# Scores of two attention stages: fp32 products on 64 rows become two fp32r products on 128 rows, with queries and keys stored as rounded part and remainder

## The chip, the cores and the metric

The program runs on one core of a Trainium2 chip, as one launch. The time is device microseconds of that launch, the median of several runs. The core has TensorE (PE, matmuls; PEld is its weight loads), VectorE (DVE), ScalarE (ACT), GpSimd (POOL), SyncE (SP), and 16 DMA engines that serve the queues of SP and POOL. SBUF has 128 partitions, of which TensorE contracts over up to 128 (its rows); PSUM takes the products.

## The reference, cut to what matters

The whole is a chain of layers over 1024 tokens and a context of 256 (1280 together). The change lies in the first mixer, which has two kinds of attention with heads of 64:

```python
# A: 8 query heads, 2 key heads (4 queries share a key head), a window of +-128 tokens plus the context, a sink column
s = einsum(qg, k) * 64**-0.5 ; s = where(valid, s, -1e30)
p = softmax(concat([s, sink]))[..., :-1] ; out = p @ v
# B: 4 heads, each two softmaxes over all 1280 keys
w = softmax(q1 @ k1.T * 64**-0.5) - lam * softmax(q2 @ k2.T * 64**-0.5) ; out = w @ v
```

q and k are normalised per head (RMS), gained, and rotated (RoPE) before. The context's own tokens attend to the context alone.

## The kernel before, in words

**project_even** (line 626 on) multiplies the normalised input with the weights, 80 steps of 24 matmuls of 128x416 (8 blocks of columns, 10 tiles of 128 tokens). Beside it, per tile i from step 33 + 4i on (`turn_at`), a side job makes q and k: SP loads 26 heads back (`qk`), ACT squares them, DVE reduces, normalises, gains and rotates them (into one of two buffers `rot`), PE transposes 14 chunks of 128x128 at step `turn_at(i) + 6` into PSUM (`pt`), ACT copies them to `stage` (L773, `copy_out`) at the next tile's `turn_at + 3`, and SP stores `stage` to DRAM as `rT` (L726, `out_stage`) at `turn_at` of the tile after. `stage` has 14 chunks because the two key heads of A are written twice, so that each stands on both partition halves. SP also loads in each step a slab of another weight (L736), which DVE multiplies and adds (L867, L870, `terms`), and stores the step's result (L753). Each queue runs in program order.

**attention_even** (line 914 on) runs 70 units: six for the two context tiles (`dac`, `wac`), then 32 pairs of `da` (kind B, one head of one tile of 128 queries: two score rows of 1280 keys) and `wa` (kind A, two heads: 384 near keys with a mask added by a product, and 256 context keys). At its start SP and POOL load keys `KA`, `KB`, values `va`, `vb` and queries `qT`, all of them for the whole sequence and with 128 partitions a DMA: the even head of a pair lies on partitions 0 to 63, the odd one on 64 to 127. A score product (L1261, L1273, L1279 to L1282, L1291) is an fp32 matmul over 64 rows; two heads on the two halves stand in turn. PE's order by hand, for unit u: transposes of exp'd scores of unit u-2 (`turn`, L1301), products with the values (`multiply`, L1324), and in between the scores of u (`score`), in two parts. `da` writes its scores into both PSUM tiles `pS`, part 0 (keys 0 to 512) before the first transposes of u-2 and part 1 (the rest) behind them; `wa` uses `pS[0]` alone, both parts behind the first transposes. Score part 0 of `wa` waits for the exp of the `da` before it to have read `pS[0]` (`expd`), and that of `da` for the first exp of `wa`. DVE takes the maxima (L1131, L1137), ACT the exp (L1083, L1088) and the copies of the transposes out of PSUM (L1108). On ACT the three copies of u-2 stand ahead of the exps of u.

In PE's waits, unit 0 needs `kb_ctx_in` and `q_ctx_in`, unit 6 (the first `da` of the sequence) `keys_in` and `q0_in`, unit 7 `ka_in`. POOL's side job (sums, L1040, L1047) begins when `q1_in` has come.

The later stage forgetting_attention (line 2662 on, tiles `fx_`) is not touched by the change; it already makes scores as two fp32r products on 128 rows (L2857, L2858), and it loads `fx_ks`, `fx_qc` and `fx_kc` by DMAs of 64 partitions with rows of 4 KB (L2735 to L2737).

Of the kernel before, what the change touches and what calls it, by code (L numbers as in the profile page):

```python
# [11 lines left out]
P = 128  # L12
D = 1024
KD = D // P
SEQ = 1024
# [610 lines left out]
def project_even(nc, a, g, hT, raw, first, p0, rT, sums):  # L626
# [29 lines left out]
    with Phase(nc, "p0") as ph:  # L656
# [8 lines left out]
        rot = [ph.sb(f"rotated{s}", [P, 28, HD]) for s in range(2)]  # L665
        ss = ph.sb("ss", [P, QK_HEADS])
        rt = ph.sb("rt", [P, QK_HEADS])
        stage = ph.sb("stage", [P, 14, P])
# [7 lines left out]
        small, squared, summed, rooted, recips, normed, gained, spread, rotated, turned, evac, stage_out = ph.sems(  # L676
            "small squared summed rooted recips normed gained spread rotated turned evac stage_out")
# [11 lines left out]
        with nc.Block() as block:  # L689
# [15 lines left out]
            def _(sp):  # L705
# [53 lines left out]
                sp.wait_ge(stage_out, 16 * n_all)  # L759
# [3 lines left out]
            def _(act):  # L763
# [5 lines left out]
                def copy_out(i):  # L769
                    act.wait_ge(turned, i + 1)  # L770
                    if i:
                        act.wait_ge(stage_out, 16 * i)
                    act.activation(stage[:, :, :], pt[:, 0:14, :], ACT.Copy).then_inc(evac, 1)  # L773

                def side():
                    for i in range(n_all):
# [3 lines left out]
                        if i >= 2:  # L780
                            act.wait_ge(turned, i - 1)
                        act.activation(rot[s][:, 0:QK_HEADS, :], qk[s][:, :, :], ACT.Square).then_inc(squared, 1)
# [25 lines left out]
            def _(dve):  # L808
# [6 lines left out]
                def side():  # L815
                    for i in range(n_all):
# [5 lines left out]
                        dve.tensor_reduce(ss[:, :], rot[s][:, 0:QK_HEADS, :], AX.X, ALU.add).then_inc(summed, 1)  # L822
# [13 lines left out]
                        if i:  # L836
                            dve.wait_ge(rotated, i)
                        cos = rope[:, 0, i:i + 1, :]
                        dve.tensor_tensor(rot[s][:, 0:8, :], qk[s][:, 0:8, :], cos.broadcast_to([P, 8, HD]), ALU.mult)
                        for y in range(2):  # L840
                            dve.tensor_tensor(rot[s][:, 8:12, :].rearrange("p (k r) d -> p k r d", r=2)[:, :, y, :],
                                              qk[s][:, 8:10, :], cos.broadcast_to([P, 2, HD]), ALU.mult)
                        dve.tensor_tensor(rot[s][:, 12:28, :], qk[s][:, 10:26, :], cos.broadcast_to([P, 16, HD]), ALU.mult)
# [9 lines left out]
                        dve.tensor_tensor(rot[s][:, 0:8, :], rot[s][:, 0:8, :], tmp[:, 0:8, :], ALU.add)  # L853
                        for y in range(2):
                            keys = rot[s][:, 8:12, :].rearrange("p (k r) d -> p k r d", r=2)[:, :, y, :]
                            dve.tensor_tensor(keys, keys, tmp[:, 8:10, :], ALU.add)
                        dve.tensor_tensor(rot[s][:, 12:28, :], rot[s][:, 12:28, :], tmp[:, 10:26, :], ALU.add).then_inc(rotated, 1)
# [26 lines left out]
            def _(pe):  # L884
                def side():
                    for i in range(n_all):
                        yield turn_at(i) + 6
                        pe.wait_ge(rotated, i + 1)
                        if i:
                            pe.wait_ge(evac, i)  # L890
                        for c, at in enumerate((0, 1, 2, 3, 8, 9, 4, 5, 6, 7, 10, 11, 12, 13)):
                            mm = pe.transpose(pt[:, at, :], rot[i % 2][:, 2 * c:2 * c + 2, :].rearrange("p h d -> p (h d)"), g.ident[:, :])
                        mm.then_inc(turned, 1)
# [20 lines left out]
def attention_even(nc, a, g, rT, p0, o_dram, sums):  # L914
# [10 lines left out]
    QA, KA_AT, QB, KB_AT = 0, 8, 4, 10  # L925
# [34 lines left out]
    with Phase(nc, "att") as ph:  # L960
        qT = ph.sb("qT", [P, KD, ALLT])
        KA = ph.sb("KA", [P, 2, P + ALLT])
        KB = ph.sb("KB", [P, 4, ALLT])
# [25 lines left out]
        (small, padded, cast, signed, scores, banked, topped, negmax, expd, sink_in, sinked, joined, summed, recips, ratioed,  # L989
         weights, turned, evac, values, o_done) = ph.sems(  # L990
            "small padded cast signed scores banked topped negmax expd sink_in sinked joined summed recips ratioed "
# [5 lines left out]
        keys_in, vb_in, ka_in, va_in, q0_in, q1_in = ph.sems("keys_in vb_in ka_in va_in q0_in q1_in")  # L997
        kb_ctx_in, ka_ctx_in, q_ctx_in, vb_ctx_in, va_ctx_in = ph.sems("kb_ctx_in ka_ctx_in q_ctx_in vb_ctx_in va_ctx_in")
# [8 lines left out]
        with nc.Block() as block:  # L1007
            @block.sync
            def _(sp):
                sp.dma_start(KB[:, :, SEQ:], rT[KB_AT:KB_AT + 4, :, SEQ:].rearrange("c p t -> p c t")).then_inc(kb_ctx_in, 16)  # L1010
                sp.dma_start(KA[:, :, P + SEQ:], rT[KA_AT:KA_AT + 2, :, SEQ:].rearrange("c p t -> p c t")).then_inc(ka_ctx_in, 16)
                sp.dma_start(vb[:, NT:, :], p0[SEQ:, V_B:V_B + 512].rearrange("(t p) d -> p t d", p=P)).then_inc(vb_ctx_in, 16)
                sp.dma_start(va[:, 1 + NT:, :], p0[SEQ:, 640:768].rearrange("(t p) d -> p t d", p=P)).then_inc(va_ctx_in, 16)
                sp.dma_start(KB[:, :, 0:SEQ], rT[KB_AT:KB_AT + 4, :, 0:SEQ].rearrange("c p t -> p c t")).then_inc(keys_in, 16)
                sp.dma_start(vb[:, 0:NT, :], p0[0:SEQ, V_B:V_B + 512].rearrange("(t p) d -> p t d", p=P)).then_inc(vb_in, 16)
                sp.dma_start(va[:, 1:1 + NT, :], p0[0:SEQ, 640:768].rearrange("(t p) d -> p t d", p=P)).then_inc(va_in, 16)
                sp.dma_start(qT[:, :, 2 * P:SEQ], rT[0:8, :, 2 * P:SEQ].rearrange("c p t -> p c t")).then_inc(q1_in, 16)
                for tile in tiles_in_order:
                    sp.wait_ge(o_done, last_of[tile] + 1)
# [5 lines left out]
            def _(pool):  # L1025
                for h in (slice(QB, QB + 4), slice(QA, QA + 4)):
                    pool.dma_start(qT[:, h, SEQ:], rT[h, :, SEQ:].rearrange("c p t -> p c t")).then_inc(q_ctx_in, 16)
# [3 lines left out]
                pool.dma_start(qT[:, :, 0:2 * P], rT[0:8, :, 0:2 * P].rearrange("c p t -> p c t")).then_inc(q0_in, 16)  # L1031
                pool.dma_start(KA[:, :, P:P + SEQ], rT[KA_AT:KA_AT + 2, :, 0:SEQ].rearrange("c p t -> p c t")).then_inc(ka_in, 16)
                pool.memset(va[:, 0, :], 0.0).then_inc(padded, 1)
                pool.memset(KA[:, :, 0:P], 0.0).then_inc(padded, 1)
# [24 lines left out]
                pool.wait_ge(q1_in, 16)  # L1059
# [183 lines left out]
            def _(pe):  # L1243
                warm_up(pe, g, po, 20)
                def score(u, part):
# [11 lines left out]
                    q = slice(P * token_tile(u), P * token_tile(u) + P)  # L1257
                    if kind == "da":
                        for c0, c1 in ((0, 512),) if part == 0 else ((512, 1024), (1024, ALLT)):
                            for m, half in enumerate(halves):  # L1260
                                mm = pe.matmul(pS[m][:, c0:c1], qT[half, QB + j, q], KB[half, j, c0:c1], start=True, stop=True)  # L1261
                                if c1 == ALLT:
                                    mm.then_inc(scores, 1)
                    elif kind == "wa":
# [4 lines left out]
                        left = [qT[half, QA + j, q] for half in halves]  # L1269
                        right = [KA[half, kv, :] for half in halves]  # L1270
                        if part == 0:
                            for e in range(2):
                                pe.matmul(pS[0][:, KEYS * e:KEYS * e + W3], left[e], right[e][:, near], start=True, stop=False)  # L1273
                            for e in range(2):
                                edges = pS[0][:, KEYS * e:KEYS * e + W3].rearrange("p (b k) -> p b k", b=3)[:, 0:3:2, :]
                                mm = pe.matmul(edges, unit_r[:, :], mask[:, which, :, :], start=False, stop=True)
                            mm.then_inc(banked, 1)
                            return
                        pe.matmul(pS[0][:, W3:512], left[0], right[0][:, far:far + P], start=True, stop=True)  # L1279
# [2808 lines left out]
```

## Time and profile before

| | us |
|---|---|
| median of 3 runs | 3462.72 (3462.21 to 3463.39) |
| span of the profiled execution | 3460.9 |
| PE busy in it | 3176.7 (92%) |
| DVE / ACT / POOL busy | 1711.3 (49%) / 1221.1 (35%) / 298.4 (9%) |

The span runs from the first to the last instruction of one profiled execution; what the runs count beyond it is 1.8 us by their median. project_even ends and attention_even begins at about 459 us, the first unit of the sequence is at 504.8 us and the last ends at about 890 us. A busy share is an average over stages; matmul records overlap in time, so the distance from one start to the next tells the cost and not the duration.

### The profile page before, as it was taken

How to read it: one execution, taken by the hardware profiler on the slowest of the kernel's cores; microseconds unless marked ns; L12 is line 12 of the kernel's file. 1: busy time of each engine (PE TensorE's matmuls, PEld its weight loads, DVE VectorE, ACT ScalarE, POOL GpSimd, SP SyncE). 2: the span in 40 equal slices, each digit the busy share in tenths (PEclk: the TensorE clock that was granted, in tenths of full speed). 3: DMA queues.
4: the chain of work that ended last, by engine and by line, in shares of the span. 5: the costliest groups of instructions: out<-in, count | busy, mean ns of one | idle time of the engine just before them, and what ended most of it. 6: DMA issues, size and time to landing. Idle time of an engine off the chain costs nothing. (4 is left out here: it accounts for less than half of the span.)

```text
span 3460.9 us, 51322 instructions
## 1 busy us (share of the span) xinstructions
PE 3176.7 (92%) x20902; PEld 2807.3 (81%) x20902; DVE 1711.3 (49%) x2697; ACT 1221.1 (35%) x2257; POOL 298.4 (9%) x357
## 2 busy tenths in 40 slices
PE   7999979999798999897999997979988999999988
PEld 4999967777587999775888976767856999999877
DVE  3459736666472211265526216746645445454343
ACT  4313235666562343124534114544423111111232
POOL 1000011100010000111211100002200000000010
PEclk9999999999899999998999998989999999999999
DMA  5556560000443221234211335110022111112332
GB/s 185 162 179 226 182 215 20 25 13 13 159 156 95 79 78 60 99 119 143 102 47 41 93 99 138 38 7 2 3 86 79 49 48 42 48 46 73 99 133 92
DMA packets 199262, 309.34 MB, mean 89 GB/s; under 512 B 43016, under 2 KB 133896, under 8 KB 197020
## 3 DMA queue, kind: packets, MB, share of 16 engines
q1 hardware_dynamic: 178448, 232.54, 21.1%
q0 software_dynamic: 20624, 74.13, 6.6%
q8 instruction: 136, 2.23, 0.3%
q14 instruction: 54, 0.44, 0.0%
HBM read 229.80 MB, written 76.81 MB: 89 GB/s over the span
## 5 line engine op out<-in xcount | busy, mean ns | idle before, releaser
L115 PE MATMUL p_pb<-p_w_hi,h_hi 128*128 128x416 f32 (+2 forms) x1168 | 408.2, 349 | 12.2 <-DVE p_w_lo L110 6.8
L116 PE MATMUL p_pb<-p_w_lo,h_hi 128*128 128x416 f32 (+2 forms) x1168 | 403.9, 346 | 0.0
L117 PE MATMUL p_pb<-p_w_hi,h_lo 128*128 128x416 f32 (+2 forms) x1168 | 403.8, 346 | 0.0
L115 PE MATMUL fu_pf<-h_hi,fu_w_hi 128*128 128x344 f32 (+1 forms) x1056 | 339.5, 322 | 8.7 <-DVE fu_pf L3747 8.7
L116 PE MATMUL fu_pf<-h_lo,fu_w_hi 128*128 128x344 f32 (+1 forms) x1056 | 340.5, 322 | 0.0
L117 PE MATMUL fu_pf<-h_hi,fu_w_lo 128*128 128x344 f32 (+1 forms) x1056 | 338.9, 321 | 0.0
L115 PEld LDWEIGHTS p_pb<-p_w_hi,h_hi 128*128 128x128 f32 x1168 | 221.0, 189 | 13.9 <-issue 12.6
L116 PEld LDWEIGHTS p_pb<-p_w_lo,h_hi 128*128 128x128 f32 x1168 | 220.7, 189 | 1.5
L117 PEld LDWEIGHTS p_pb<-p_w_hi,h_lo 128*128 128x128 f32 x1168 | 220.4, 189 | 1.3
L115 PEld LDWEIGHTS fu_pf<-h_hi,fu_w_hi 128*128 128x128 f32 x1056 | 199.9, 189 | 9.1 <-DVE fu_pf L3747 9.1
L117 PEld LDWEIGHTS fu_pf<-h_hi,fu_w_lo 128*128 128x128 f32 x1056 | 199.9, 189 | 0.0
L116 PEld LDWEIGHTS fu_pf<-h_lo,fu_w_hi 128*128 128x128 f32 x1056 | 199.7, 189 | 0.0
L142 ACT ACTIVATE fu_w_hi<-fu_raw 128x512 fp32r<-128x512 f32 x88 | 50.9, 624 | 351.8 <-PE fu_pf L117 343.0
L3756 DVE TENSOR_SCALAR fu_f<-fu_pf,taps 128x1026 f32<-128x1026 f32 x44 | 56.6, 1286 | 224.7 <-PE fu_pf L117 224.7
L1108 ACT ACTIVATE att_ET<-att_pT 128x512 f32<-128x512 f32 (+1 forms) x204 | 108.0, 529 | 159.7 <-PE att_pT L1301 159.7
L115 PE MATMUL s_pb<-h_hi,s_w_hi 128*128 128x348 f32 (+1 forms) x480 | 158.7, 331 | 4.3 <-DVE s_w_lo L110 4.3
L116 PE MATMUL s_pb<-h_lo,s_w_hi 128*128 128x348 f32 (+1 forms) x480 | 155.7, 324 | 0.0
L117 PE MATMUL s_pb<-h_hi,s_w_lo 128*128 128x348 f32 (+1 forms) x480 | 155.6, 324 | 0.0
L115 PE MATMUL fd_po<-fd_w_hi,fd_fs_hi 128*128 128x512 f32 x352 | 139.2, 395 | 9.3 <-DVE fd_fs_lo L110 9.3
L116 PE MATMUL fd_po<-fd_w_lo,fd_fs_hi 128*128 128x512 f32 x352 | 138.5, 393 | 0.0
L117 PE MATMUL fd_po<-fd_w_hi,fd_fs_lo 128*128 128x512 f32 x352 | 138.4, 393 | 0.0
L1131 DVE TENSOR_REDUCE att_mx<-att_pS 128x1 f32<-128x1280 f32 x64 | 95.1, 1486 | 79.9 <-PE att_pS L1261 79.9
(555 smaller groups left out, 6948.9 us busy)
## 6 DMA issues: line engine op xcount, KB each, us to landing
fu_raw<-in_ffn_up SPq DMA_DIRECT2D x88, 256.0 KB, 3.1
fd_raw<-in_ffn_down SPq DMA_DIRECT2D x44, 512.0 KB, 3.6
p_slab<-in_adaln_w SPq DMA_DIRECT2D x64, 256.0 KB, 3.3
la_qkv<-p SPq DMA_DIRECT2D x16, 1024.0 KB, 5.0
p<-p_o SPq DMA_DIRECT2D x60, 208.0 KB, 2.1
s_raw<-in_w_in POOLq DMA_DIRECT2D x48, 256.0 KB, 3.7
rT<-p_stage SPq DMA_DIRECT2D x10, 896.0 KB, 5.2
p_raw<-in_ab_w_in POOLq DMA_DIRECT2D x10, 832.0 KB, 7.2
```

Source lines behind the costliest of these rows:

```text
L115: pe.matmul(out, left[0], right[0], start=start, stop=False)
L116: pe.matmul(out, left[0], right[1], start=False, stop=False)
L117: return pe.matmul(out, left[1], right[0], start=False, stop=stop)
L142: eng.activation(self.slots[s][0][:, self.half * h:self.half * h + self.half, :], self.raw[h][:, :, :], ACT.Copy).then_inc(self.hi_done[h], 1)
L1108: act.activation(ET[:, k0:k1, :], pT[:, 0:k1 - k0, :], ACT.Copy).then_inc(evac, 1)
L1131: dve.tensor_reduce(mx[s][:, m:m + 1], pS[m][:, 0:ALLT], AX.X, ALU.max).then_inc(topped, 1)
L3756: ch.link(dve.tensor_scalar(f[e][:, :, :], pf[e][:, :, 2:FFN_CUT + 2], taps[2], None, ALU.mult))
```

## The change: what it does

1. `rT` holds two parts, the fp32r-rounded value and the remainder, each of 13 chunks (the second copy of A's keys goes). ACT writes the rounded part from PSUM, DVE the remainder behind it (`low_out`), and SP stores both: two DMAs of 832 KB for one of 896 KB.
2. DVE rotates in one product and one sum over 26 heads where it had four and four; one `rot` buffer for two, so DVE waits for the transposes of the tile before; ACT squares into `tmp`. PE makes 13 transposes for 14.
3. The keys lie in SBUF as rounded part on partitions 0 to 63 and remainder on 64 to 127. The queries lie twice, with the rounded part on both halves and the remainder on both halves, and for one tile of tokens in each of two buffers. One score is two fp32r products on 128 rows: q_hi with (k_hi, k_lo), then q_lo with the same.
4. All these loads are DMAs of 64 partitions on SP's queue: two for a set of keys, four for eight heads of queries of one tile, in rows of 512 B. SP loads tiles 2 and on when the scores of the tile two before are done. POOL loads none of them and starts its side job on `va_in`.
5. `banked` goes.

```diff
@@ project_even
-                    sp.dma_start(rT[:, :, i * P:i * P + P].rearrange("c p t -> p c t"), stage[:, :, :]).then_inc(stage_out, 16)
+                    for part in range(2):
+                        sp.dma_start(rT[part, :, :, i * P:i * P + P].rearrange("c p t -> p c t"), stage[part][:, :, :].bitcast(F32)).then_inc(stage_out, 16)
...
-                    act.activation(stage[:, :, :], pt[:, 0:14, :], ACT.Copy).then_inc(evac, 1)
+                    act.activation(stage[0][:, :, :], pt[:, 0:QK_HEADS // 2, :], ACT.Copy).then_inc(staged, 1)
...
+                        dve.tensor_tensor(rot[:, :, :], rot[:, :, :], tmp[:, :, :], ALU.add).then_inc(rotated, 1)
+                        if i:
+                            low_out(i - 1)
...
+                def low_out(i):
+                    dve.wait_ge(staged, i + 1)
+                    lo_part(dve, stage[1][:, :, :], pt[:, 0:QK_HEADS // 2, :], stage[0][:, :, :]).then_inc(evac, 1)
@@ attention_even
+                def load_keys(keys, at, chunks, tokens, came):
+                    for part, half in enumerate(halves):
+                        sp.dma_start(keys[half, :, at:at + tokens.stop - tokens.start].bitcast(F32),
+                                     rT[part, chunks, :, tokens].rearrange("c (e d) t -> d (c e) t", d=HD)).then_inc(came, 16)
+
+                def load_queries(tile, first, chunk, came):
+                    for part in range(2):
+                        for half in halves:
+                            sp.dma_start(Q[ring[tile] % 2][half, first:first + 8, part, :].bitcast(F32),
+                                         rT[part, chunk:chunk + 4, :, P * tile:P * tile + P].rearrange("c (e d) t -> d (c e) t", d=HD)
+                                         ).then_inc(came[ring[tile] % 2], 16)
...
+                load_keys(KB, SEQ, kb_at, ctx, kb_ctx_in)
+                load_queries(NT, A_HEADS, QB, qb_in)
+                load_keys(KA, P + SEQ, ka_at, ctx, ka_ctx_in)
+                load_queries(NT, 0, QA, qa_in)
+                load_queries(NT + 1, A_HEADS, QB, qb_in)
                 sp.dma_start(vb[:, NT:, :], ...)
                 sp.dma_start(va[:, 1 + NT:, :], ...)
+                load_queries(NT + 1, 0, QA, qa_in)
+                load_keys(KB, 0, kb_at, seq, keys_in)
+                load_keys(KA, P, ka_at, seq, ka_in)
                 sp.dma_start(vb[:, 0:NT, :], ...)
                 sp.dma_start(va[:, 1:1 + NT, :], ...)
                 for tile in tiles_in_order:
+                    if ring[tile] + 2 < len(tiles_in_order):
+                        after = tiles_in_order[ring[tile] + 2]
+                        sp.wait_ge(scores, exps_before[last_of[tile] + 1])
+                        load_queries(after, A_HEADS, QB, qb_in)
+                        load_queries(after, 0, QA, qa_in)
                     sp.wait_ge(o_done, last_of[tile] + 1)
...
+                    def whole(out, head, keys, stop):
+                        queries = Q[ring[token_tile(u)] % 2]
+                        pe.matmul(out, queries[:, head, 0, :], keys, start=True, stop=False)
+                        return pe.matmul(out, queries[:, head, 1, :], keys, start=False, stop=stop)
...
-                            for m, half in enumerate(halves):
-                                mm = pe.matmul(pS[m][:, c0:c1], qT[half, QB + j, q], KB[half, j, c0:c1], start=True, stop=True)
+                            for m in range(2):
+                                mm = whole(pS[m][:, c0:c1], A_HEADS + 2 * j + m, KB[:, 2 * j + m, c0:c1], True)
```

## Rows read from the trace of the kernel before

**Rows 1.** Windows: length, busy (count) per engine, granted clock, DMA share, GB/s.
```profile
505.00:890.00 385.00, 378.68 (x2713) 282.55 (x2712) 252.45 (x460) 234.12 (x479) 35.37 (x29) 1.00 0.06 20
...
230.00:350.00 120.00, 120.00 (x667) 118.74 (x667) 110.13 (x153) 38.43 (x47) 3.00 (x4) 1.00 0.64 209
```

**Rows 2.** Timeline of PE, one pair of units: start us, us, instruction.
```profile
649.12 1.13 PE L1261 MATMUL att_pS<-att_KB,att_qT 64*128 64x512 f32 x4
650.18 0.66 PE L1301 MATMUL att_pT<-ident,att_E 128*128 128x128 f32 x4
650.77 1.56 PE L1261 MATMUL att_pS<-att_KB,att_qT 64*128 64x512 f32 x8
652.26 0.66 PE L1301 MATMUL att_pT<-ident,att_E 128*128 128x128 f32 x4
...
655.82 0.92 PE L1273 MATMUL att_pS<-att_KA,att_qT 64*128 64x384 f32 x4
...
657.74 0.66 PE L1301 MATMUL att_pT<-ident,att_E 128*128 128x128 f32 x4
...
660.77 0.70 PE L1261 MATMUL att_pS<-att_KB,att_qT 64*128 64x512 f32 x2
```

**Rows 3.** Timeline of ACT in the same pair.
```profile
654.08 0.38 ACT L1108 ACTIVATE att_ET<-att_pT 128x256 f32<-128x256 f32 x1 [0.53 <-PE att_pT L1301]
654.36 1.32 ACT L1083 ACTIVATE att_E<-att_pS,att_nm 128x1280 f32<-128x1280 f32 x1
```

**Rows 4.** Timeline of PE in forgetting_attention, fp32r scores between fp32 products.
```profile
2206.93 0.66 PE L2872 MATMUL fx_pT<-ident,fx_E 128*128 128x128 f32 x4 [0.96 <-DVE fx_E L2824]
2207.34 0.38 PE L2857 MATMUL fx_pS<-fx_ks,fx_qs 128*128 128x272 f32 x1
2207.56 0.29 PE L2858 MATMUL fx_pS<-fx_kc,fx_qc 128*128 128x272 f32 x1
2207.68 0.60 PE L2872 MATMUL fx_pT<-ident,fx_E 128*128 128x128 f32 x4
...
2212.93 0.28 PE L2858 MATMUL fx_pS<-fx_kc,fx_qc 128*128 128x144 f32 x1
2213.04 0.51 PE L2872 MATMUL fx_pT<-ident,fx_E 128*128 128x128 f32 x3
```

**Rows 5.** Timeline of PE in a stream of fp32r products, 512 columns.
```profile
1024.10 0.39 PE L117 MATMUL c_po<-c_w_hi,c_hc_lo 128*128 128x512 f32 x1
1024.33 0.39 PE L115 MATMUL c_po<-c_w_hi,c_hc_hi 128*128 128x512 f32 x1
```

**Rows 6.** Windows, DMA share and GB/s last: start of forgetting_attention, start of attention_even.
```profile
2088.00:2094.00 6.00, 0.86 (x4) 0.66 (x2) 1.69 (x3) 2.50 (x3) 0.00 (x0) 0.50 1.04 208
2095.00:2100.00 5.00, 1.08 (x3) 0.35 (x2) 1.59 (x7) 0.36 (x2) 0.00 (x0) 0.50 1.05 394
2101.00:2106.00 5.00, 5.00 (x30) 4.69 (x28) 1.59 (x4) 2.48 (x5) 0.00 (x0) 0.66 1.03 221
...
470.00:495.00 25.00, 16.20 (x105) 12.86 (x102) 13.88 (x32) 14.59 (x55) 0.00 (x0) 0.81 1.04 382
```

**Rows 7.** Timeline of PE: first scores of the stage, and of unit 6.
```profile
469.06 3.50 PE L1291 MATMUL att_pS<-att_KB,att_qT 64*128 64x256 f32 x16 [3.81 <-DMA att_qT<-rT]
...
504.78 1.13 PE L1261 MATMUL att_pS<-att_KB,att_qT 64*128 64x512 f32 x4 [0.81 <-ACT att_E L1097]
```

**Rows 8.** Timelines of DVE and PE in project_even: last sum of a tile, its transposes.
```profile
290.15 1.22 DVE L857 TENSOR_TENSOR p_rotated<-p_rotated,p_tmp 128x1024 f32<-128x1024 f32 x1
...
297.74 1.69 PE L892 MATMUL p_pt<-ident,p_rotated 128*128 128x128 f32 x14
```

**Rows 9.** Groups of DVE in 230 to 350 us: busy us, mean ns, idle before.
```profile
L110 DVE TENSOR_TENSOR p_w_lo<-p_raw,p_w_hi 128x1664 fp32r<-128x1664 f32 x4 | 7.4, 1882 | 0.0
L857 DVE TENSOR_TENSOR p_rotated<-p_rotated,p_tmp 128x1024 f32<-128x1024 f32 x6 | 7.3, 1215 | 0.0
```

**Rows 10.** DMA issues of the page: count, KB each, us to landing.
```profile
rT<-p_stage SPq DMA_DIRECT2D x10, 896.0 KB, 5.2
```

More of the change, by code:

```diff
@@ L664, in project_even @@
         tmp = ph.sb("tmp", [P, QK_HEADS, HD])
-        rot = [ph.sb(f"rotated{s}", [P, 28, HD]) for s in range(2)]
+        rot = ph.sb("rotated", [P, QK_HEADS, HD])
         ss = ph.sb("ss", [P, QK_HEADS])
         rt = ph.sb("rt", [P, QK_HEADS])
-        stage = ph.sb("stage", [P, 14, P])
+        stage = ph.pair("stage", [P, QK_HEADS // 2, P])
         slab = [ph.sb(f"slab{s}", [P, MOD_BLK]) for s in range(2)]
@@ L836, in side @@
                         if i:
-                            dve.wait_ge(rotated, i)
+                            dve.wait_ge(turned, i)
                         cos = rope[:, 0, i:i + 1, :]
[L839 to L843, printed above, removed]
+                        dve.tensor_tensor(rot[:, :, :], qk[s][:, :, :], cos.broadcast_to([P, QK_HEADS, HD]), ALU.mult)
                         pairs = qk[s][:, :, :].rearrange("p h (x y m) -> p h x y m", x=2, y=2)
@@ L852, in side @@
                         dve.wait_ge(spread, i + 1)
[L853 to L857, printed above, removed]
+                        dve.tensor_tensor(rot[:, :, :], rot[:, :, :], tmp[:, :, :], ALU.add).then_inc(rotated, 1)
+                        if i:
+                            low_out(i - 1)
+                    yield turn_at(n_all - 1) + 7
+                    low_out(n_all - 1)
+                def low_out(i):
+                    dve.wait_ge(staged, i + 1)
+                    lo_part(dve, stage[1][:, :, :], pt[:, 0:QK_HEADS // 2, :], stage[0][:, :, :]).then_inc(evac, 1)
                 def terms(i, k):
@@ L960, in attention_even @@
     with Phase(nc, "att") as ph:
-        qT = ph.sb("qT", [P, KD, ALLT])
-        KA = ph.sb("KA", [P, 2, P + ALLT])
-        KB = ph.sb("KB", [P, 4, ALLT])
+        Q = [ph.ctx.enter_context(nc.sbuf_tensor(f"att_Q{b}", [P, A_HEADS + 2 * B_HEADS, 2, P], F32R)) for b in range(2)]
+        KA = ph.ctx.enter_context(nc.sbuf_tensor("att_KA", [P, 2, P + ALLT], F32R))
+        KB = ph.ctx.enter_context(nc.sbuf_tensor("att_KB", [P, 2 * B_HEADS, ALLT], F32R))
         va = ph.sb("va", [P, 1 + NT + NC, P])
@@ L1286, in score @@
                             if kind == "dac":
[L1287 removed]
+                                mm = whole(pS[e][:, CTX * h:CTX * h + CTX], A_HEADS + i, KB[:, i, SEQ:], True)
                             else:
                                 at = WAC + CTX * h
[L1290 to L1291 removed]
+                                mm = whole(pS[e][:, at:at + CTX], 4 * j + i, KA[:, j, P + SEQ:], True)
                         mm.then_inc(scores, 2)
```

79 lines of the change are left out of this document (31 added, 48 removed).

## The prediction

> **What bounds the kernel now.** I read the page first: PE is busy for 3176.7 of 3460.9 us, so a change counts only where PE waits for something or issues less. Then the windows of the two stages that the change touches. In the sequence part of attention_even PE is busy for 378.7 of 385 us, DVE for 252.5 and ACT for 234.1; in project_even, from 230 to 350 us, PE is busy all the time, but DVE too for 110.1 of 120 [rows 1]. The start of attention_even is another matter: its first unit waits for its queries, and the DMA engines are full from 470 to 495 us at 382 GB/s; the first `da` begins at 504.78 [rows 6, 7]. Last I read the timeline of one pair of units and, for prices, the stage that already works in the new way.
>
> The pair: from 649.12 to the same place at 660.77 is 11.65 us, 32 times [rows 2]. `da` part 0 holds PE from 649.12 to 650.18, 1.06 us. Part 1 begins 0.17 us after its four transposes should be through (650.18 + 0.42) and ends at 652.26: 1.66 us. `wa`, both parts, runs from 655.82 to 657.74: 1.92 us. That is 4.64 us of scores in 11.65. Behind 652.26 stands a chain that does not get shorter: transposes, copy on ACT at 654.08, exp at 654.36 as soon as the copy is nearly out, scores of `wa` at 655.82 [rows 2, 3]. So 655.82 is set by ACT's queue, 3.56 us after 652.26, and PE has a quarter of a microsecond of idle time ahead of it.
>
> **Scores in the pair.** An fp32r product of 512 columns behind another one costs 0.23 us [rows 5]. One of 272 costs 0.12 (2207.56 to 2207.68), one of 144 costs 0.11 (2212.93 to 2213.04), and the first behind fp32 work costs 0.22 for 272, which is 0.10 more [rows 4]; four transposes cost 0.41 there, as here. So no drain shows between the two kinds but this 0.1, and below 144 columns I take 0.11. New counts: part 0 is four of 512: 0.32 + 3 x 0.226 = 1.00 us. Part 1 is four of 512 and four of 256: 1.00 + 4 x 0.12 = 1.48. `wa` is four of 384 (0.17, the first 0.27), two masks of 256 (0.12), four of 128 (0.11) and two of 256 (0.12): 0.78 + 0.24 + 0.44 + 0.24 = 1.70. Saved: 0.06 + 0.18 + 0.22 = 0.46 us a pair. It is little, since the fp32 products on the two halves run side by side: two heads of 512 in fp32 take about what four fp32r products of 512 take.
>
> Who is late next: ACT's copy and exp still stand 3.56 us behind the end of part 1, so that wait stays. Behind `wa` the maxima start a little later against PE's next transposes, since the last product is one of 256 and nothing drains behind it; I take 0.04 us off. That leaves 0.42 x 32 = **13.4 us saved**. Bounds: if the waits on ACT (0.24 and some 0.1) went as well, 0.83 x 32 = 27 us; if the chains through DVE and ACT took back all but a quarter of the gain, 3 us.
>
> **Loads at the start.** Here the change adds most. With rows of bytes as in the code: keys of B for the context 1.05 MB, queries of one tile and kind 1.05 MB, keys of B for the sequence 4.19 MB, of A 1.05 MB and 0.26 MB. Unit 6 needs the keys and the B queries of tile 0, and these stand last on SP's queue, behind everything: 5 x 1.05 + 0.26 + 4.19 + 1.05 + 1.05 = 11.8 MB by DMAs of 64 partitions and 3.3 MB of values by DMAs of 128, with 0.4 MB of masks on POOL's queue. The trace has a price for each kind: in forgetting_attention, loads of 64 partitions (260 KB each, rows of 4 KB) keep the DMA engines as full as any, but move 208 and 221 GB/s, and the value load of 128 partitions between them moves 394 [rows 6]; I take 216. Then 11.8 / 0.216 = 54.6 us and 3.7 / 0.38 = 9.8 us. The first bytes of the stage come at about 460.6, so the queries of tile 0 land at 525, and unit 6 starts at about 526 and not at 504.8: **+21 us**. The context units end at about 508 (the first starts at about 471.5, having 2.1 MB to wait for) and can't cover it. PE then idles for some 17 us and begins unit 6 at the lower clock; the first scores of this stage after a pause took 3.50 us for 16 records of 256 columns [rows 7], more than the 12 records of up to 512 columns in parts 0 and 1 at the full clock (2.72), so I add 1.5 us. Bounds: at 382 GB/s for all, 15.5 MB take 41 us and unit 6 starts at 503 to 505, cost 0; at 180 GB/s for the 64-partition loads (rows of 512 B where the trace has 4 KB) 65.6 + 9.8 us, unit 6 at 537, +32.
>
> Two pages of the Trainium skill disagree here. "DMA: Bandwidth & Descriptors", section "Anatomy of one DMA — SWDGE (gpsimd) path", prices a transfer at 2 us and bytes at 436 GB/s and knows nothing of partitions; by it 15.5 MB land in 38 us, before the context units end, and the change would keep its gain (the second rival below). "SBUF — State Buffer", section "Door 1: The DMA port swizzle", says that 64 consecutive partitions reach 8 of 16 ports, which by its figures is 218 GB/s. The trace's 208 against 394 speaks for the second.
>
> In the steady part a tile needs 2.1 MB of queries in about 45 us, 10 us at 216 GB/s, issued two tiles ahead: hidden, as the DMA engines stand at 0.06 there [rows 1]. If it weren't, each tile would pay what is over 45 us. SP's stores of `o` stand behind those issues; the buffer is wanted a tile later. POOL's side job starts some 25 us later and has its first deadline three units after unit 6. Waits added on PE (`qa_in`, `qb_in`) are passed two tiles ahead but at the start.
>
> **project_even.** PE: one transpose less in each of 10 tiles, 0.12 us each: -1.2 us. DVE: the remainder costs 1.88 us a tile (an fp32r difference of 1664 elements, row L110 [rows 9]); the rotation's sum in one piece saves about 0.4 against four (1215 ns for 1024 elements and 1882 for 1664 give some 0.15 us per piece), its product the same: +1.1 us net on a DVE that has 9.9 us of idle time in the six tiles of 120 us. PE's transposes now need the remainder of the tile before, which stands behind the sum. Before, the sum ended at 291.37 and the transposes came at 297.74 [rows 8], so 6.4 us of cover, of which the remainder takes 1.9 and a lag of DVE that grows by up to 1 us a tile the rest. SP waits for the remainder and then issues two stores where it had one; one took 5.2 us to land [rows 10], so the slab behind it lands about 3 us later, and DVE waits for slabs. What is queued behind SP's wait: the next slab, the store of the step's result (four buffers, 18 us of cover). I take 1.4 us of PE stall: **+0.2 us** with the transposes. Bounds: -1.2, and +8 if the cover is gone from the second tile on and DVE's surplus of about 1 us a tile, plus a late slab, goes to PE. The lower granted clock does not come in: PE stays busy.
>
> **Sum.** 3460.9 + 21 + 1.5 - 13.4 + 0.2 = 3470.2 us of span; the median of the runs lies 1.8 above the span of the profiled execution, so 3472.
>
> **Rivals.** (1) *The start's loads are slow and the steady gain is large*: PE's waits on ACT vanish too, 27 us saved; 3462.7 + 22.5 - 27 + 0.2 = 3458. For it: 0.24 us of PE idle per pair might shrink if exp can start earlier. Against: the exp starts with the end of ACT's copy, which hangs on PE's own transposes. (2) *The start's loads hide*: SP's DMAs to the two halves overlap, or 64 partitions are not the cause of 208 GB/s; unit 6 starts at 505 to 508. 3462.7 + 2 - 13.4 + 0.2 = 3451.5, faster. Against: the window of `fx_ks` also alternates halves and stays at 208 to 221. (3) *DVE becomes the bound in project_even*: from the tile at which DVE's lag passes 4.5 us (6.4 less 1.9), PE waits for it in each tile of the dense part; +8 instead of +0.2, on top of the start: 3480. For it: 110.1 of 120 us. Against: from 350 us on the side work is halved. This and the forecast lie on the slow side, (2) on the fast side, and decides at about 350 GB/s for the 64-partition loads. That the two products don't save at all (the change doesn't do what it says) is the lower bound of the pair: 3 us saved, 3482.
>
> **How the numbers follow.** Forecast 0.53, rival 1 0.17, rival 2 0.13, rival 3 and no saving together 0.17. Within the forecast the time is 3464 to 3480 as the rate goes from 240 to 195 GB/s. A measurement of this kernel tells 0.2%, 6.9 us, from no change: below 3455.8 is faster, above 3469.6 slower. Slower: 0.17 and about three quarters of the forecast, 0.58. Faster: rival 2 and a little of rival 1, 0.14. The same: 0.28. The range for 8 in 10 leaves out rival 2 and the far end of 3: 3455 to 3486.
>
> **What would show it.** The first L1261 of unit 6 at 521 to 530 us with the DMA share at 1 and about 216 GB/s while keys and queries load; at 505 to 508 the forecast is wrong. Pairs of 11.2 us, not 10.8 (rival 1) or 11.6. L892 in project_even ahead of which PE has no idle time, or little, at 337 us; tens of stalls there would be rival 3. PE's clock at the lower level just after 526.

## The result: slower, 3486.4 us for 3463.1

| | before | after |
|---|---|---|
| median of 4 runs each, us | 3463.05 (3462.21 to 3465.98) | 3486.38 (3483.45 to 3491.09) |
| ratio, 95% interval | | 1.0067 [1.0053, 1.0081] |
| span of the profiled execution | 3460.9 | 3481.6 |
| SP's first load of attention_even | 458.88 | 457.83 |
| first score (unit 0) | 469.06 | 475.19 |
| first score of unit 6 | 504.78 | 536.30 |
| first score of unit 7, the first `wa` | 511.21 | 545.83 |
| first score of the last `wa` | 882.50 | 907.50 |

The forecast was 3472.0 in 3455 to 3486: the sign is right, the size isn't. The table gives the account. Up to unit 6 the new kernel loses 31.5 us, from there to unit 7 another 3.1, over the 31 pairs that follow it wins 9.6 (371.3 to 361.7), and in what comes behind, where nothing was changed, this one execution is 4.3 us shorter: 3460.9 + 31.5 + 3.1 - 9.6 - 4.3 = 3481.6. The medians lie 23.3 us apart, the profiled executions 20.7. One of e6's twelve runs below took 5270 us at a granted clock of 0.55 and is left out; no other run was like it.

Windows of the kernel after, to be read against [rows 1, 6]; the last three columns are granted clock, DMA share and GB/s:

```profile
230.00:350.00 120.00, 120.00 (x665) 118.73 (x664) 108.78 (x116) 36.85 (x46) 3.00 (x4) 1.00 0.71 231
350.00:400.00 50.00, 50.00 (x283) 49.36 (x282) 48.41 (x49) 16.21 (x20) 0.00 (x0) 1.00 0.72 227
545.00:908.00 363.00, 355.37 (x2633) 324.70 (x2634) 244.66 (x444) 226.29 (x465) 35.28 (x27) 1.00 0.28 60
470.00:500.00 30.00, 15.39 (x86) 14.27 (x87) 11.25 (x23) 11.51 (x45) 0.00 (x0) 0.68 1.15 205
500.00:515.00 15.00, 11.98 (x76) 11.15 (x75) 7.08 (x21) 8.84 (x31) 0.00 (x0) 0.77 1.04 205
520.00:525.00 5.00, 0.00 (x0) 0.00 (x0) 0.00 (x0) 0.00 (x0) 0.00 (x0) 0.50 1.04 363
530.00:535.00 5.00, 0.00 (x0) 0.00 (x0) 0.00 (x0) 0.00 (x0) 1.08 (x2) 0.50 1.14 196
```

The DMA engines are as full as before (share over 1) and move 205 GB/s where they moved 382 in [rows 6]. Only while the values of the sequence come, whose DMAs have 128 partitions, do they move 363. In project_even PE is busy for 120.00 of 120 us with DVE at 108.8, and for 50.00 of 50 where DVE is fullest, at 48.4 (350 to 400 us; before it had 43.9 there).

PE's timeline at the places of [rows 7]: unit 0, unit 6, and the transposes ahead of unit 7's scores.

```profile
475.19 0.58 PE L1280 MATMUL att_pS<-att_KB,att_Q 128*128 128x256 f32 x1 [10.99 <-DMA att_Q<-rT]
...
536.30 0.80 PE L1280 MATMUL att_pS<-att_KB,att_Q 128*128 128x512 f32 x1 [21.73 <-DMA att_Q<-rT]
...
537.32 0.63 PE L1280 MATMUL att_pS<-att_KB,att_Q 128*128 128x512 f32 x1
537.74 0.63 PE L1281 MATMUL att_pS<-att_KB,att_Q 128*128 128x512 f32 x1
...
545.42 0.66 PE L1320 MATMUL att_pT<-ident,att_E 128*128 128x128 f32 x4 [2.04 <-DMA att_Q<-rT]
545.83 0.42 PE L1280 MATMUL att_pS<-att_KA,att_Q 128*128 128x384 f32 x1
```

PE stands 21.73 us for the queries, its scores then lie 0.42 us apart at the lower clock, and before unit 7 it waits for queries once more. One pair in the steady part, against [rows 2]:

```profile
674.42 0.44 PE L1280 MATMUL att_pS<-att_KA,att_Q 128*128 128x384 f32 x1
...
676.22 0.66 PE L1320 MATMUL att_pT<-ident,att_E 128*128 128x128 f32 x4
...
679.34 0.47 PE L1280 MATMUL att_pS<-att_KB,att_Q 128*128 128x512 f32 x1
...
680.35 0.60 PE L1320 MATMUL att_pT<-ident,att_E 128*128 128x128 f32 x4
680.70 0.48 PE L1280 MATMUL att_pS<-att_KB,att_Q 128*128 128x512 f32 x1
...
682.19 0.60 PE L1320 MATMUL att_pT<-ident,att_E 128*128 128x128 f32 x4
...
685.70 0.45 PE L1280 MATMUL att_pS<-att_KA,att_Q 128*128 128x384 f32 x1
```

From 674.42 to 685.70 is 11.28 us, for 11.65 before. `wa` holds PE for 1.80 us, part 0 for 1.01, part 1 for 1.49. ACT's part, against [rows 3], is the same: a copy of 0.38 us, and the exp 0.28 us behind its start.

```profile
660.22 0.38 ACT L1129 ACTIVATE att_ET<-att_pT 128x256 f32<-128x256 f32 x1 [0.53 <-PE att_pT L1320]
660.50 1.32 ACT L1104 ACTIVATE att_E<-att_pS,att_nm 128x1280 f32<-128x1280 f32 x1
```

And the new work on DVE in project_even, groups from 230 to 350 us, against [rows 9]:

```profile
L850 DVE TENSOR_TENSOR p_rotated<-p_rotated,p_tmp 128x1664 f32<-128x1664 f32 x5 | 9.4, 1883 | 0.0
L110 DVE TENSOR_TENSOR p_stage_lo<-p_pt,p_stage_hi 128x1664 fp32r<-128x1664 f32 x4 | 7.5, 1882 | 0.0
```

### The profile page after: what moved, and what is told of

Read it like the earlier page. It is cut to its first block and busy times, and to the rows that moved or that the text cites. A ratio compares the mean times of both kernels' runs of the same rounds, so it can differ in the third digit from the quotient of the medians.

```text
span 3481.6 us, 51340 instructions
## 1 busy us (share of the span) xinstructions
PE 3162.1 (91%) x20892; PEld 2860.8 (82%) x20892; DVE 1722.4 (49%) x2647; ACT 1220.1 (35%) x2257; POOL 295.9 (8%) x353
## 5 line engine op out<-in xcount | busy, mean ns | idle before, releaser
L115 PE MATMUL p_pb<-p_w_hi,h_hi 128*128 128x416 f32 (+2 forms) x1168 | 407.7, 349 | 12.8 <-DVE p_w_lo L110 7.5
L115 PEld LDWEIGHTS p_pb<-p_w_hi,h_hi 128*128 128x128 f32 x1168 | 221.0, 189 | 14.4 <-issue 13.3
```

The source lines that it names most:

```text
L115: pe.matmul(out, left[0], right[0], start=start, stop=False)
```

## Experiments

In all eleven experiments I looked for the same places. "Unit 6" is its first score counted from SP's first load of the stage, since the stage itself begins at 454.6 to 458.9 from one execution to the next. "Pairs" is the first `wa` to the last. "Rest" is the last `wa` to the end of the span: the same code in all. The ratio of each experiment is to runs of before on the same chip, whose median was 3461.5 to 3462.8.

| kernel | unit 6 | pairs | rest | median | ratio to before [95%] |
|---|---|---|---|---|---|
| before | 45.9 | 371.3 | 2578.4 | 3463.1 | 1 |
| after | 78.5 | 361.7 | 2574.1 | 3486.4 | 1.0067 [1.0053, 1.0081] |
| e1 before, halves | 48.1 | 374.3 | 2579.0 | 3468.6 | 1.0019 [1.0009, 1.0028] |
| e2 full width | 51.0 | 361.7 | 2574.2 | 3452.6 | 0.9975 [0.9966, 0.9985] |
| e3 values last | 68.4 | 368.5 | 2576.2 | 3482.2 | 1.0057 [1.0035, 1.0080] |
| e4 sums late | 77.6 | 368.6 | 2575.7 | 3485.3 | 1.0059 [1.0041, 1.0077] |
| e5 interleaved | 51.3 | 360.1 | 2579.7 | 3459.2 | 0.9990 [0.9982, 0.9999] |
| e6 stacked | 50.8 | 361.7 | 2581.4 | 3456.7 | 0.9983 [0.9973, 0.9993] |
| e7 values last, sums early | 72.3 | 361.8 | 2575.6 | 3477.0 | 1.0043 [1.0026, 1.0059] |
| e8 kept busy | 78.3 | 361.6 | 2578.0 | 3486.4 | 1.0072 [1.0055, 1.0089] |
| e9 interleaved, reordered | 50.2 | 361.7 | 2582.3 | 3456.7 | 0.9979 [0.9970, 0.9988] |
| e10 sums late, split later | 77.1 | 360.5 | 2580.9 | 3485.3 | 1.0057 [1.0042, 1.0072] |
| e11 kept busy longer | 78.6 | 364.7 | 2577.9 | 3484.7 | 1.0063 [1.0044, 1.0081] |

The rest moves by 8 us. For the same 15816 matmul records PE is busy for 2341 us in the shortest (after) and 2354 in the longest (e9), with a granted clock of 0.96 and 0.95: at least part of it is slower matmuls, and why they differ stays open. So one profile can't show an end-to-end difference of a few us; places inside the stage can.

### e1: is it the partitions? The kernel before, its loads cut in two

All loads from `rT`, on SP and on POOL, as the one shown:

```diff
+                def by_halves(eng, dst, src, came):
+                    for half in halves:
+                        eng.dma_start(dst[half], src[:, half, :].rearrange("c p t -> p c t")).then_inc(came, 16)
-                sp.dma_start(KB[:, :, 0:SEQ], rT[KB_AT:KB_AT + 4, :, 0:SEQ].rearrange("c p t -> p c t")).then_inc(keys_in, 16)
+                by_halves(sp, KB[:, :, 0:SEQ], rT[KB_AT:KB_AT + 4, :, 0:SEQ], keys_in)
...
```

> The kernel before (fp32 scores, 3463), with every load from rT cut into two DMAs of 64 partitions: the same bytes, the same rows of 512 B and 4 KB. Nothing of the change is in it. Theory (64 partitions alone make the loads slow): until about 517 us the core moves 200 to 220 GB/s instead of 318 to 403 in the windows from 460 to 495 us, with the DMA share at 1 all the same; the loads end at about 517 and not 497; unit 6's first score comes at 506 to 514 instead of 504.8, and the kernel takes 3464 to 3472. Rival A (what is slow after the change is its bytes, its order or its short rows, not the partitions): 360 to 390 GB/s, loads through at 497 to 500, 3463. Rival B (DMAs to the two halves from two queues overlap): between the two, 280 GB/s or more.

Windows, and unit 6:

```profile
470.00:495.00 25.00, 15.22 (x98) 12.41 (x100) 13.54 (x31) 13.80 (x55) 0.00 (x0) 0.80 1.04 247
500.00:512.00 12.00, 9.90 (x71) 7.47 (x72) 5.36 (x11) 5.67 (x18) 0.00 (x0) 1.00 1.05 203
```
```profile
506.25 1.13 PE L1269 MATMUL att_pS<-att_KB,att_qT 64*128 64x512 f32 x4 [0.81 <-ACT att_E L1105]
```

382 GB/s has become 247 with the values among them and 203 without, by one edit: 64 partitions a DMA instead of 128. The loads end at about 517 us. Rival A falls. So does B: both queues have had loads of both halves under way since 465 us, and from 473 to 480 us the core moves 211. The theory holds as far as this goes; e5 narrows it. The fp32 kernel loses only 0.2% by it, since it has about 6 MB of keys, queries and context values to bring ahead of unit 6 where the changed one has 15.5.

Of its 6.6 us, 2.2 are lost ahead of unit 0, which comes 12.6 us after the first load for 10.2; unit 6 waits for ACT alone, as before. Another 3.0 are one pair, the second, of 15.88 us for 12.87. POOL's sums hang on the last of these loads, come late, and their split falls beside DVE's work on that pair: L1171 takes 1.48 us for 0.22. More on this under e4.

### e2: the changed kernel with DMAs of 128 partitions

```diff
-                    for part, half in enumerate(halves):
-                        sp.dma_start(keys[half, :, at:at + tokens.stop - tokens.start].bitcast(F32), rT[part, chunks, :, tokens].rearrange("c (e d) t -> d (c e) t", d=HD))
+                    for part in range(2):
+                        sp.dma_start(keys[:, n * part:n * part + n, at:at + tokens.stop - tokens.start].bitcast(F32), rT[part, chunks, :, tokens].rearrange("c p t -> p c t"))
```

> The changed kernel with as many DMAs of the same bytes and the same row lengths for keys and queries, but each over all 128 partitions; what they bring is not what the scores want (rounded parts of two heads in the place of part and remainder), so the attention is computed of wrong numbers, and all else stays. Theory (partition count): 340 to 400 GB/s in the start, unit 6's first score at 503 to 507 instead of 536.3, the pairs stay at 11.26, and the kernel takes 3450 to 3455, faster than before. Rival A (the bytes, or unit 6's queries last on the queue, make it late): unit 6 at 525 to 536, 3475 to 3486. Rival C (the scores are the loss, not the start): over 3463 in spite of an early unit 6.

```profile
465.00:475.00 10.00, 4.90 (x24) 4.44 (x24) 2.53 (x3) 1.20 (x5) 0.00 (x0) 0.79 1.11 295
...
485.00:495.00 10.00, 6.43 (x54) 5.91 (x53) 6.29 (x18) 7.29 (x27) 0.00 (x0) 1.00 1.03 403
```
```profile
505.56 0.80 PE L1281 MATMUL att_pS<-att_KB,att_Q 128*128 128x512 f32 x1 [3.23 <-DMA att_Q<-rT]
```

Unit 6 comes 27.5 us sooner after the first load than in the changed kernel (51.0 for 78.5), the pairs take the same 361.7, and the kernel is faster than before (its scores are wrong, so it tells the time alone). Rivals A and C fall: neither the bytes nor the new scores are the loss.

### e5: the same 64 partitions, but every second one

```diff
-        halves = [slice(0, 64), slice(64, 128)]
+        halves = [slice(0, P, 2), slice(1, P, 2)]
```

> The changed kernel with one line other: the two parts lie on the even and the odd partitions instead of on 0 to 63 and 64 to 127 (a product sums over the rows in any order, so the scores are the same). Every load has still 64 partitions, the same bytes, rows and order. Theory (a load is slow because its 64 partitions lie in one half of the 128, and so reach half of what receives them): 330 to 400 GB/s in the start, unit 6 at 503 to 507 instead of 536.3, pairs of 11.26, 3450 to 3456: faster than before. Rival G (the number of partitions in a DMA counts, wherever they lie): 200 GB/s, unit 6 at 534 to 537, 3484 to 3487.

```profile
465.00:475.00 10.00, 4.28 (x21) 4.08 (x22) 1.56 (x2) 0.00 (x0) 0.00 (x0) 0.66 1.13 292
...
485.00:495.00 10.00, 7.13 (x59) 6.84 (x60) 6.09 (x16) 8.15 (x29) 0.00 (x0) 1.00 1.02 409
```
```profile
507.42 0.80 PE L1280 MATMUL att_pS<-att_KB,att_Q 128*128 128x512 f32 x1 [2.82 <-DMA att_Q<-rT]
```

One line turns 205 GB/s into 292 for the queries (rows of 512 B) and 409 for the keys (rows of 4 KB), and 1.0067 into 0.9990. Rival G falls: it isn't the number of partitions but that they lie together in one half. The 292 isn't owed to the alternate partitions, since e2 moves 295 over all 128 in the same window; the queries' DMAs have short rows and are also small (256 KB), and no run separates the two. Unit 6 came 0.4 us later than I gave it; 3459 misses the expected 3450 to 3456. Against e2 the start and the pairs are as good; the difference lies in the rest (2579.7 for 2574.2), where PE is busy for 2348.8 us and 2341.6.

The Trainium skill has this in "SBUF — State Buffer", section "Door 1: The DMA port swizzle": which of 16 ports a partition uses hangs on bits of its number, and 0 to 63 reach eight of them. By its formula every second partition reaches all. The page's section "Can I just issue two DMAs to hit both halves?" says that only one transfer over all 128 partitions can do so; there this run differs, with 409 GB/s for 64.

### e6: rT stored so that loads are 128 wide

```diff
-        rT = scratch("rT", (2, QK_HEADS // 2, P, ALLT))
+        rT = scratch("rT", (QK_HEADS, HD, 2, ALLT))
...
+                        sp.dma_start(here[:, h, 0, :].bitcast(F32), heads[h, :, :, tokens].rearrange("h d s t -> (d s) h t"))
...
+                        sp.dma_start(here[s:P:2, :, 1, :].bitcast(F32), heads[:, :, 1 - s, tokens].rearrange("h d t -> d h t"))
```

> The changed kernel with rT laid out as head, dimension, part, token, so that keys and the first copy of the queries come in DMAs of 128 partitions (dimension and part together) with the same number of DMAs and bytes; the second copy of the queries, remainder above part, comes by two DMAs of 64 alternate partitions each. Scores are the same four products, summed in another pairing. The stores of project_even stay 128 partitions wide, but their rows of 512 B now lie 10 KB apart. Theory: as with the interleaved one, unit 6 at 503 to 507, 3450 to 3456; and if alternate partitions turn out slow (Rival G) this one still gains for keys and half of the queries: unit 6 at 508 to 514, 3457 to 3463. The pair stays at 11.26 under both.

```profile
509.17 0.47 PE L1285 MATMUL att_pS<-att_KB,att_Q 128*128 128x512 f32 x1 [0.81 <-ACT att_E L1123]
```

Unit 6 at 509.2 is 50.8 us after the first load (this stage began at 458.4), 2.2 us later than I gave it, and 3456.7 is 0.7 us over: as good as e5 within the intervals. Unit 6 waits only for ACT, 0.81 us as before, so no more is to be had by width.

### e3, e7, e4, e10: what stands ahead of unit 6, and a gain given back

e3 moves the two value loads of the sequence behind the queries of tile 0 (in SP's loop over the tiles):

```diff
+                    if ring[tile] == 0:
+                        sp.dma_start(vb[:, 0:NT, :], p0[0:SEQ, V_B:V_B + 512].rearrange("(t p) d -> p t d", p=P)).then_inc(vb_in, 16)
+                        sp.dma_start(va[:, 1:1 + NT, :], p0[0:SEQ, 640:768].rearrange("(t p) d -> p t d", p=P)).then_inc(va_in, 16)
```

e7 adds the first of these to e3, e4 is the second alone, and e10 adds the third to e4:

```diff
-                pool.wait_ge(va_in, 16)
+                pool.wait_ge(keys_in, 32)
```
```diff
-                pool.wait_ge(va_in, 16)
+                pool.wait_ge(scores, exps_before[8])
```
```diff
                         pool.wait_ge(pressed, i)
+                        pool.wait_ge(geared, i)
```

> The changed kernel with the two value loads of the sequence (2.1 and 0.5 MB of 128 partitions, 7 us of DMA time) behind the queries of tile 0 instead of ahead of them; POOL's loads of the sums, which wait for these values, move back with them. Theory (the start is bound by what the DMA queue has to bring ahead of unit 6's queries): unit 6 at 528 to 530 instead of 536.3, its queries for unit 7 in time (no wait ahead of unit 7, 2 us), POOL's sums no longer beside them: 3476 to 3479. Rival D (something else holds unit 6, such as the context units or a wait of SP's): unit 6 at 534 or later, 3484 to 3487. Rival E (the values come too late and the gain is given back two units on): unit 6 at 529, but a wait for values in unit 8 and 3482 or more.

> The changed kernel with POOL's first two loads of the sums (0.5 MB each) held until unit 7's scores are through, instead of starting when the values of A are in, beside the queries of tile 0. Theory (they compete): unit 6 at 534 to 535 instead of 536.3, the wait ahead of unit 7 (2.0 us) gone or under 1 us, 3482 to 3484. Rival F (they have room beside a load of 64 partitions, since they go to all 128): no change, 3485 to 3487. If the press at unit 9 then waits for POOL, that shows as a wait on acc_lo and the gain is given back.

> The run with the values behind the queries of tile 0, but POOL's first loads of the sums now wait only for the keys of B (about 514 us) instead of the values of A. In the run before this one unit 6 came 10 us earlier and 7 us of it were given back two units on: PE waited 5.4 us for POOL's acc_lo ahead of the press, since the sums came only at 541 to 550. Theory (the press's deadline took the gain): unit 6 at 528 to 531 (the sums' 1 MB now lies ahead of the queries), no wait ahead of the press, the second pair 12.5 instead of 19.3, 3476 to 3480. Rival (the gain goes elsewhere, to the late values): the second pair stays above 14, 3482 or more.

> The run with the late sums, plus one wait on POOL: its second split (cast and difference of the next sums) starts only when DVE has added the row of the press before. In the run with the late sums alone unit 6 was 1.8 us earlier and the second pair took 19.4 us instead of 12.5: DVE's L1196 took 3.64 us there, with POOL's 2.34 us difference beside it, where it takes 1.55 us alone, and PE waited 4.1 us for the row. Theory (a DVE operation of this kind stands still while POOL's difference runs): with the wait L1196 takes 1.55 us again, the second pair 12.5 to 14.5 us, 3478 to 3482, faster with one wait more. Rival (the second pair is long because the sums are late as such): it stays at 17 us or more, 3485.

PE in e3: unit 6, and the press two units on.

```profile
526.13 0.79 PE L1281 MATMUL att_pS<-att_KB,att_Q 128*128 128x512 f32 x1 [13.13 <-DMA att_Q<-rT]
...
554.21 0.59 PE L1361 MATMUL att_pS<-att_acc_hi,att_pick 128*2 128x512 f32 x1 [5.43 <-POOL att_acc_lo L110]
```

PE in e7, with the wait for the queries still ahead of it:

```profile
529.66 0.80 PE L1281 MATMUL att_pS<-att_KB,att_Q 128*128 128x512 f32 x1 [18.00 <-DMA att_Q<-rT]
```

e3's unit 6 gained 10.1 us, more than the 7 of the values, but its second pair took 19.3 us for 12.5. I had expected a late value load, if anything; it was POOL's sums, which hang on the same load (the 5.43 us of wait above, and the lower clock behind it, 0.50 from 555 to 558 us). e7 lets them start sooner: unit 6 wins 6.2 us, the pair is 12.46 us, and the median is 3477.0, inside the expected 3476 to 3480, though its five runs spread from 3471 to 3483.

e4's unit 6 wins 0.9 us and the wait ahead of unit 7 goes, so the sums do compete with the queries, by little. The median doesn't tell (3485.3), for its second pair is 19.4 us too. Its timelines of DVE and POOL, then PE:

```profile
555.06 2.35 POOL L110 TENSOR_TENSOR att_acc_lo<-att_acc,att_acc_hi 128x1024 fp32r<-128x1024 f32 x1
...
555.32 2.11 DVE L1184 SCALAR_TENSOR_TENSOR att_ratio<-att_l,neglam,att_r 128x1 f32<-128x1 f32 x1
...
559.81 2.34 POOL L110 TENSOR_TENSOR att_acc_lo<-att_acc,att_acc_hi 128x1024 fp32r<-128x1024 f32 x1
559.86 3.64 DVE L1196 SCALAR_TENSOR_TENSOR att_E<-att_E,att_ratio 128x1280 f32<-128x1280 f32 x1
...
564.20 0.76 PE L1280 MATMUL att_pS<-att_KB,att_Q 128*128 128x512 f32 x1 [4.14 <-DVE att_later L1242]
```

L1184 takes 0.22 us elsewhere and here 2.11, until POOL's difference is through at 557.4; L1196 takes 1.55 and here 3.64. PE waits 4.14 us, and behind that it runs at the lower clock (0.51 from 563 to 570 us), which is part of the pair's 19.4. e10 holds POOL back until DVE has added the row:

```profile
559.89 1.55 DVE L1197 SCALAR_TENSOR_TENSOR att_E<-att_E,att_ratio 128x1280 f32<-128x1280 f32 x1
```
```profile
562.13 0.47 PE L1281 MATMUL att_pS<-att_KB,att_Q 128*128 128x512 f32 x1 [1.15 <-DVE att_later L1243]
```

L1196 (here L1197) is back at 1.55, the second pair at 13.3: shown in the trace. The time doesn't show it: 3485.3 for both, where 3478 to 3482 was expected; the profile of e10 has 8.1 us less in the pairs (6.1 in this one, 2.0 in a later one) and 5.1 more in the rest. The two small operations beside POOL's first difference stay slow (L1185 1.42 us), and PE still waits 1.15. Whether e4's other executions have the collision at all, which hangs on tenths of a us, stays open.

The Trainium skill, "SBUF — State Buffer", section "Who interferes with whom", says that a DVE instruction with two SBUF inputs can't run beside a GpSimd instruction that reads SBUF; these rows agree.

### e8 and e11: the clock at unit 6

```diff
+                        if u == 6:
+                            pe.wait_ge(expd, exps_before[6])
+                            warm_up(pe, g, pS[0], 85)
```

e11 has 98 for 85. Each product gives two records in the trace.

> The changed kernel with 85 products of the identity (0.22 to 0.26 us each) on PE while it waits for unit 6's queries, so that PE isn't idle for 21.7 us. Theory (the pause costs the lower clock besides the wait): the granted clock is at 1.0 at unit 6, a 512-column score costs 0.23 and not 0.43 us, unit 6 to 7 takes 6.4 to 7.5 us and not 9.5 (the queries of unit 7 land late all the same), and 1 to 2 us are saved: 3484 to 3486. Rival (the clock costs nothing, the DMA hides it): the last pairs come as late as after, 3486 to 3487. If the 85 outlast the queries, unit 6 comes later than 536.3 by what they outlast.

> The run that keeps PE busy ahead of unit 6, with 98 products instead of 85: the 85 ended 3.2 us before the queries came, and the granted clock was down again. Theory (the pause alone takes the clock down): idle time ahead of unit 6 under 1.5 us, the first 512-column scores 0.23 us behind each other and not 0.43, unit 6's part 1 through 2 us earlier; the time is then held by the queries of unit 7 (they land about 8 us after unit 6's), so no more than 0.5 to 1.5 us is saved at the end. Rival (the clock is down there for another reason): 0.43 us a score in spite of it.

e8's 85 products ended 3.18 us before the queries came and the scores were at the lower clock all the same: it settled nothing. e11:

```profile
512.50 22.15 PE L237 MATMUL att_pS<-ident 128*128 128x128 f32 x196 [0.72 <-ACT att_E L1118]
534.83 0.50 PE L1280 MATMUL att_pS<-att_KB,att_Q 128*128 128x512 f32 x1 [0.18 <-DMA att_Q<-rT]
535.17 0.40 PE L1281 MATMUL att_pS<-att_KB,att_Q 128*128 128x512 f32 x1
535.41 0.40 PE L1280 MATMUL att_pS<-att_KB,att_Q 128*128 128x512 f32 x1
...
542.76 1.12 PE L1320 MATMUL att_pT<-ident,att_E 128*128 128x128 f32 x4 [2.64 <-DMA att_Q<-rT]
543.52 0.67 PE L1280 MATMUL att_pS<-att_KA,att_Q 128*128 128x384 f32 x1
```

With 0.18 us of pause the scores are 0.24 us apart and not 0.42. But PE only arrives earlier at the next wait, 2.64 us for unit 7's queries, and the clock falls there: the first pair took 15.8 us for 11.1. In the profile the second `wa` comes 103.1 us after the first load, for 99.1 in the changed kernel, so the gain is lost again; the medians, 3484.7 of two runs for 3486.4, can't tell 0.5 to 1.5 us. The clock's price is real, and here a transfer hides it.

### e9: the two together

> The interleaved kernel (parts on even and odd partitions) with the queries of tile 0 ahead of the two value loads of the sequence, and POOL's first sums held only until the keys of B are in. In the interleaved kernel unit 6 waited 2.8 us for its queries (507.4), and its first scores then cost 0.43 us instead of 0.23. Theory: the queries are issued at about 494, when the scores of the last unit that used their buffer are through, and land before 502; no wait ahead of unit 6 but that for ACT, unit 6 at 503 to 505, unit 7 6.4 us behind it instead of 7.5, and 3452 to 3456 where the interleaved one takes 3459: the fastest so far. Rival (SP's wait for that buffer is now what holds the queries): they land after 504, the wait stays at 2 us or more, and the time is the same as the interleaved one's.

It is e5 and e7 in one. Unit 6, and a window just behind it:

```profile
508.77 0.47 PE L1281 MATMUL att_pS<-att_KB,att_Q 128*128 128x512 f32 x1 [1.94 <-ACT att_E L1119]
```
```profile
510.00:512.00 2.00, 2.00 (x8) 1.78 (x7) 0.00 (x0) 0.60 (x1) 0.00 (x0) 0.50 1.05 401
```

The queries are in time, as the theory has it, and ACT is what unit 6 waits for, 1.94 us. It comes at 508.8 and not at 503 to 505: the stage began at 458.5, and from the first score to unit 6 go 37.0 us for before's 35.7. The clock still falls behind that pause, from 1.0 to 0.5 (of 2.4 GHz to 1.2), and unit 7 comes 7.6 us behind, not 6.4. The median, 3456.7, just over what I gave, is 6 us under before's in the same runs and with e6's the lowest of the kernels that keep the computation, but e5, e6 and e9 can't be told apart.

## Why the prediction was wrong, step by step

**The start's loads: right in kind, too small.** This step failed. I had +21 us from 216 GB/s for DMAs of 64 partitions, and it was 32.6 from the first load to unit 6 (78.5 for 45.9); unit 6 came 78.5 us after the first load where the sum says 67.1 (526 less 458.9). Of the 11.4 us: the 11.8 MB went at 205 and, in the first ten us, at about 180, not 216 (some 4 us); I had priced the context's values and the masks, 1.1 MB, at 380, but they lie between and in the same 205 (1.1 / 0.205 - 1.1 / 0.38, 2.5 us); POOL's sums ran beside the queries (0.9 by e4, 1.4 by e10). That leaves some 3.5 us open. The windows from the first load to unit 6 add up to 16.2 MB in e4, which has no sums there, for 15.5 in the working; 0.7 MB at 205 GB/s would be 3.4 us, but which transfers they are isn't traced. The rate itself lay inside the forecast's spread of 240 to 195 GB/s (from two windows of one stage): 205 alone adds 2.9 us, to 3475. What carried the result out of the range is mostly what the sum left out, with 3.4 us in the pairs and 1.6 in the clock. The upper bound of the step, 537 at 180 GB/s, is 78.1 us from the first load and was just reached. PE stood 21.7 us and not 17, with the context units through at 514.6 and not 508. It was the right mechanism: e1 and e2 show the cause from both sides, e5 names it exactly.

**The clock, +1.5: 3.1.** From unit 6 to unit 7 went 9.5 us for 6.4. The lower clock costs some 2.1 to 2.2: e3 and e4, at the lower clock and without a wait for unit 7's queries, take 8.1 and 8.2, where e6, with the clock at 1.00, takes 6.0. The new scores give 0.4 of it back. The rest, 1.4, is a wait that the working left out: the A queries of tile 0 come behind the B ones, 1.05 MB at 200 GB/s are 5.2 us.

**The pair, -0.42: -0.37.** Parts 0 and 1 are as worked out (1.01 and 1.49 for 1.00 and 1.48), `wa` takes 1.80 for 1.70. The wait for ACT stayed, so rival 1 falls. A pair with a press saves 0.41. One pair of 14.4 us near the end, 12.8 in e5, took 1.6 back. That is the clock again: both executions have the same wait of 1.2 us ahead of the `da` in it, and only in the first does the granted clock fall behind it. In all 9.6 for 13.0 over 31 pairs. After, then e5:

```profile
809.00:811.00 2.00, 1.67 (x6) 1.32 (x7) 0.52 (x2) 0.00 (x0) 0.52 (x1) 0.72 0.04 10
811.00:813.00 2.00, 2.00 (x8) 1.71 (x7) 0.00 (x0) 0.60 (x1) 0.00 (x0) 0.50 0.00 0
...
778.00:780.00 2.00, 1.61 (x9) 1.42 (x10) 0.58 (x2) 0.00 (x0) 0.52 (x1) 1.00 0.01 2
780.00:782.00 2.00, 2.00 (x15) 1.81 (x15) 0.80 (x1) 0.72 (x2) 0.00 (x0) 1.00 0.04 8
```

Rival 1's 27 us are not the sum of its own terms: 0.42, 0.24 and 0.1 are 0.76 a pair, 24 us.

**project_even, +0.2.** The stage began 1.05 us earlier, but with this same project_even it begins anywhere from 454.6 to 458.7. DVE's busy time grew by 10.1 us over the stage (100 to 460 us: 223.2 to 233.3), as worked out at 1.1 a tile, though not in the window from 230 to 350. PE had no idle time from 150 to 440 us, so rival 3 falls; the term is nothing within 2 us.

**Queries in the steady part are hidden**, as said: 0.28 of the DMA engines, no wait but at the start.

**Rival 2**, that the loads hide, fell here; with the parts on alternate partitions it is nearly what happens: 3459 and 3457, where it said 3451.5.

## What to carry to other kernels

Before a loaded tile is put on half the partitions, work out the bytes that the first consumer needs over the rate that such DMAs show, not over the usual one. A contraction sums over its rows in any order, so the two parts can lie on alternate partitions: one line, 27 us here. When a load is moved, look at who else waits for its semaphore: the gain of e3 went there.

## What the runs showed of the hardware that I had not expected

- 64 partitions every second one: 409 GB/s in rows of 4 KB, 292 in rows of 512 B (128 partitions: 403 and 295). 64 side by side: 205 for either, so there the length of the row costs next to nothing.
- A DVE operation with two inputs in SBUF stood still until POOL's difference was through: 3.64 us for 1.55, 2.11 for 0.22 (e4). In e1 L1183 began 0.15 us ahead of that difference and took its usual 1.54, and POOL took 3.59 us for 2.35.
- The length of a pause alone doesn't tell the clock behind it. After pauses of 1.22 us (after, 809) and 1.94 (e9) the clock went to 0.50. After 1.23 (e5, the same place) and 2.04 (after, ahead of unit 7) it stayed at 1.00:

```profile
545.00:549.00 4.00, 3.58 (x30) 3.58 (x30) 1.59 (x3) 1.86 (x4) 0.00 (x0) 1.00 1.15 197
```
